# Gated recurrence, first two heads: where two weight splits stand on ScalarE, and where the second head's square sum stands on TensorE

## The reference, cut to what matters

```
def hgrn2_mixer(h, lb, w_in, o_norm, w_o):
    proj = h @ w_in
    q_x, f_x, i_x, g_x = jnp.split(proj, [HK, 2 * HK, 2 * HK + HV], axis=-1)
    f = lb + (1.0 - lb) * jax.nn.sigmoid(f_x)
    q = heads(jax.nn.silu(q_x)); k = heads(1.0 - f); log_f = heads(jnp.log(f)); v = heads(i_x)
    b = jnp.cumsum(log_f, axis=3)                    # chunks of 32 tokens
    q_rel = q * jnp.exp(b - b_ref);  k_rel = k * jnp.exp(b_ref - b)
    o_intra = (causal(q_rel k_rel^T)) v
    q_dec = q * jnp.exp(b);  k_dec = k * jnp.exp(b_last - b)
    # scan over chunks: o_inter = q_dec state; state = decay * state + k_dec^T v
    gate = silu(g_x)
    o = rms_norm(o_intra + o_inter, o_norm) * gate
    return o @ w_o
```

## Time and profile before

| | |
|---|---|
| median of 3 runs | 1789.33 us (1784.96, 1789.33, 1789.35) |
| the profiled execution | 1786.21 us |
| its span in the trace | 1784.2 us |
| PE busy | 1660.7 us, 93% of the span |
| the stretch that the change touches | 1091 to 1154 us |
| mean granted clock of PE | 0.968 of full speed |

### The profile page before, as it was taken

The page is one execution under the profiler, slowest core; times in us unless marked ns, Lnnn a source line. Parts: engine busy times, 40 slices in busy tenths (PEclk is TensorE's granted clock), DMA queues, the critical chain, the costliest instruction groups (busy, mean ns, idle before and its releaser), DMA issues.

```text
span 1784.2 us, 28711 instructions
## 1 busy us (share of the span) xinstructions
PE 1660.7 (93%) x10394; PEld 1345.7 (75%) x10394; DVE 850.8 (48%) x1463; ACT 744.1 (42%) x1149; POOL 648.7 (36%) x374
## 2 busy tenths in 40 slices
PE   5999979869889999999999999899999999999997
PEld 4787668837566668878888887788878878888885
DVE  6565868756675544532121245466664542212125
ACT  2333334323744444623142346567674622323232
POOL 5544310004421125644444453233334544444441
PEclk9999999979899999999999998799999999999997
DMA  8622210002121122233333331122222223333331
GB/s 291 194 83 74 69 37 3 4 12 83 47 60 28 33 71 83 72 95 93 98 92 105 94 104 39 48 71 59 73 69 84 59 83 94 99 91 105 94 95 59
DMA packets 250958, 140.33 MB, mean 79 GB/s; under 512 B 10122, under 2 KB 242657, under 8 KB 250865
## 3 DMA queue, kind: packets, MB, share of 16 engines
q1 hardware_dynamic: 249552, 137.12, 26.4%
q0 software_dynamic: 1008, 1.66, 0.4%
q10 hardware_dynamic: 304, 0.26, 0.0%
HBM read 136.93 MB, written 2.10 MB: 78 GB/s over the span
## 4 chain that ended last, share of the span: by engine, by line
issue 41%; PE 24%; POOL 11%; DVE 10%; ACT 5%; DVEq 4%; DMA 2%; ACTq 1%; POOLq 1%; SPq 1%
PE bank L745 13%; POOL w_low L554 10%; DVE hg_state L2046 2%; PE bank L1030 2%; DVE bank L2043 2%; PE bank L794 2%; DMA x_tok<-in_x 1%; DVEq L2479 1%; PE bank L1190 1%; PE bank L1189 1%; DVE hg_k_dec L2043 1%; DVEq L2792 1%; PE bank L1217 1%; SPq L438 1%; DVE sum_sq L2043 1%
## 5 line engine op out<-in xcount | busy, mean ns | idle before, releaser
L554 POOL TENSOR_TENSOR w_low<-w_raw,w_high 128x1024 fp32r<-128x1024 f32 (+2 forms) x218 | 517.5, 2374 | 989.7 <-ACT w_high L1476 989.6
L745 PE MATMUL bank<-act_high,w_high 128*128 128x512 f32 x976 | 392.8, 402 | 12.6 <-POOL w_low L554 10.5
L745 PE MATMUL bank<-act_low,w_high 128*128 128x512 f32 x976 | 383.5, 393 | 0.0
L745 PE MATMUL bank<-act_high,w_low 128*128 128x512 f32 x976 | 383.2, 393 | 0.0
L1476 ACT ACTIVATE w_high<-w_raw 128x1024 fp32r<-128x1024 f32 (+2 forms) x218 | 219.3, 1006 | 276.8 <-PE bank L745 265.3
L745 PEld LDWEIGHTS bank<-act_high,w_high 128*128 128x128 f32 x976 | 184.7, 189 | 66.1 <-POOL w_low L554 14.5
L745 PEld LDWEIGHTS bank<-act_high,w_low 128*128 128x128 f32 x976 | 184.7, 189 | 40.4
L745 PEld LDWEIGHTS bank<-act_low,w_high 128*128 128x128 f32 x976 | 185.0, 190 | 38.9 <-issue 2.2
L745 PE MATMUL bank<-hid_high,w_high 128*128 128x512 f32 x472 | 184.7, 391 | 3.8 <-DVE mix_out L2721 3.8
L745 PE MATMUL bank<-hid_low,w_high 128*128 128x512 f32 x472 | 184.4, 391 | 0.0
L745 PE MATMUL bank<-hid_high,w_low 128*128 128x512 f32 x472 | 184.4, 391 | 0.0
(11 more groups left out here) (566 smaller groups left out, 2869.8 us busy)
## 6 DMA issues: line engine op xcount, KB each, us to landing
w_raw<-in_mlp_w SPq DMA_DIRECT2D x128, 512.0 KB, 4.0
w_raw<-in_hgrn_w_in SPq DMA_DIRECT2D x32, 512.0 KB, 4.1
w_raw<-in_w_in SPq DMA_DIRECT2D x29, 512.0 KB, 4.0
w_ada_piece<-in_w_ada SPq DMA_DIRECT2D x5, 2048.0 KB, 16.2
w_raw<-in_w_out SPq DMA_DIRECT2D x8, 512.0 KB, 3.8
w_raw<-in_mla_w_o SPq DMA_DIRECT2D x8, 512.0 KB, 3.8
w_raw<-in_hgrn_w_o SPq DMA_DIRECT2D x8, 512.0 KB, 3.8
w_raw<-in_mla_w_in SPq DMA_DIRECT2D x6, 512.0 KB, 4.0
```

Source lines behind the costliest of these rows:

```text
L554: gp.tensor_tensor(WL[:, c0 % 2, 0:kt, 0:m], WR[:, c0 % 2, 0:kt, 0:m], WH[:, c0 % 2, 0:kt, 0:m].bitcast(F32), ALU.subtract).then_inc(w_lo, 1)
L745: mm = pe.matmul(bank[0:m, :], w[:, k, 0:m], a[:, k0 + k, :], start=(k == 0 and n_ == 0), stop=(k == kt - 1 and n_ == 2))
```

## The change

Three things are moved, and nothing is added or left out: the split of job G0+5 stands on ScalarE right behind that of G0+4, ahead of the norm's logarithm, where it stood behind the norm; the copy for G0+6 stands behind head 0's query silu, where it stood behind the five exponentials; and the square sum of head 0 stands amid job G0+7, after its first nine matmuls, where it stood behind the whole job. The loop over heads 2 to 7 is as before.

```
@@ job(c0, ..., amid=None)
                         mm = pe.matmul(bank[0:m, :], w[:, k, 0:m], a[:, k0 + k, :],
                                        start=(k == 0 and n_ == 0), stop=(k == kt - 1 and n_ == 2))
+                    if k == 2 and amid:
+                        amid()
                 mm.then_inc(job_done, 1)
@@ TensorE, hgrn(n, o, second)
-                if second:
-                    job(G0 + 3, n * 4, free["g"], n * 4 + 4)
-                if o is not None:
+                def square_sum():
                     pe.wait_ge(g_sq, o + 1)
                     pe.matmul(PB[7][:, :], ONES[:, :], OSQ[:, :], start=True, stop=True).then_inc(g_ss, 1)
+
+                if second:
+                    job(G0 + 3, n * 4, free["g"], n * 4 + 4, amid=square_sum)
+                elif o is not None:
+                    square_sum()
@@ ScalarE
             mlp(0, F0)
             high(G0 + 4)
+            high(G0 + 5)
             rstd_of(D, R1, 2)
 
             def hgrn(n, o, second=False):
 
-                if o is None:
-                    high(G0 + 5)
-                else:
+                if o is not None:
                     act.wait_ge(g_sc, o + 1)
...
                     act.activation(QG[:, :], TG[1][:, :], ACT.Silu).then_inc(g_sig, 1)
+                    if o is None:
+                        high(G0 + 6)
...
                     act.activation(GG[:, :], TG[3][:, :], ACT.Silu).then_inc(g_gate, 1)
-                if o is None:
-                    high(G0 + 6)
```

More of the change, by code:

```diff
@@ L733, in job @@
             def job(c0, r, fr, n, kt=8, m=P, hi=AH, lo=AL, k0=0, ready=None, bank=None,
-                    spare=None):
+                    spare=None, amid=None):
                 s = c0 % 2
```

## The result

The changed kernel takes 1776.51 us, the median of 4 runs (1772.66 to 1777.52), against 1787.14 us for the kernel before (4 runs, 1780.21 to 1789.35): a ratio of 0.9936, with a 95% interval from 0.9916 to 0.9957. Run again twice beside other kernels, with 12 runs each time, it gave 0.9944 [0.9926, 0.9963] and 0.9954 [0.9935, 0.9973]. As differences of medians that is 10.6, 8.6 and 7.2 us, where 8.6 was forecast.

A forecast was written before the change was run, and what follows sets the result against it. PE, busy 93% of the span, was taken to bound the kernel, through its waits and slowed clock. Terms 0.7 + 1.7 + 2.5 + 3.1 + 0.6 = 8.6 us, from 1787.5, gave 1778.9 us; range 1774 to 1785.5.

The forecast's parts named there:

- the third wait: PE's wait ahead of turning head 1's values: 2.8 us shrinks to 2.1; clock staying up gives up to 1.7.
- G0+5's start: PE starts G0+5 at 1104.7 us instead of 1105.38, released by VectorE's product instead of GpSimd's split: 0.7 us.
- the cover of the norm's table load: On ScalarE, G0+5's copy and the 1.28 us load finish before PE's sum, within 0.1 us; no cost to the norm.
- G0+5 at full clock: On PE, G0+5 takes 5.49 us instead of 7.16 behind a shorter wait: 1.7 us.
- the two nearest waits: PE's clock fell behind 2.03 us and stayed up behind 1.91, so 1.35 us ahead of G0+5 should keep it up.
- The wait ahead of G0+6: PE waits 0.9 us for GpSimd's low part instead of 3.41; G0+6 starts 2.5 us closer behind G0+5.
- G0+6 at full clock: On PE, G0+6 takes 5.49 us instead of 8.57 behind a short gap: 3.1 us.
- The square sum: Moved amid G0+7 on PE: Ln 1.0 us sooner, but VectorE's third product limits turning head 1's values: 0.6 us.
- the clock's: Rival: PE's clock falls all the same in G0+5 and G0+6; gain 6.0 us, 1781.5 us, chance 0.15.
- VectorE's last addition of squares: Rival: GpSimd's split shuts VectorE out of the norm's last addition; gain 3 to 6 us, some 1783.2 us, chance 0.08.
- The weights were there: Rival: G0+5's weights land late and its copy holds up the norm on ScalarE; slower, 1793 us, chance 0.02.
- Nothing was given back: Rival: weight loads or the loop behind the first heads take up the gain; no change, 1787.5 us, chance 0.05.

The follow-up runs named there:

- the table first: Changed kernel plus a one-column Ln on ScalarE ahead of G0+5's copy, so the norm's table loads before that copy; 0.9954 of before, 1775.72 us.
- the longer gap: Changed kernel with PE also waiting for head 0's logarithm ahead of G0+5; 1778.66 us against 1776.05 us for the changed kernel.
- the first two edits: Kernel before with G0+5's split ahead of the norm and G0+6's copy behind the silu, square sum not moved; 0.9948 of before.
- the first edit's profile: Kernel before with only G0+5's split moved ahead of the norm; 0.999 of before, 1780.84 us against 1783.15 us.
- the earlier copy: Changed kernel plus one-column Ln ahead of G0+5's copy, two VectorE products moved, G0+6's copy ahead of head 0's silu; 1771.65 us, again 1773.79 us.

## Why the prediction was right

The forecast was 8.6 us and its range held the time. The start from which the time was reckoned was partly luck: the kernel before had medians of 1787.14, 1783.15, 1783.94 and 1783.29 us in four sets of runs, and the forecast began at 1787.5. The stretch shrank by 8.5 us in one profile of the changed kernel and 9.8 in the two others; the 1.3 us between them are the clock behind the third wait, which the forecast had left to its range. By its steps:

- **G0+5's start**, 0.7 forecast, 0.33 measured. G0+5 is indeed released by VectorE's product. The step that was off is the cover of the norm's table load: the copy started at 1095.67, 0.42 us behind the end of G0+3's last matmul (1094.86 plus 0.39) and not 0.1 as reckoned. The load behind it made the norm's Ln 0.3 us late. The run with the table first gave that 0.3 back, though it also had the copy 0.3 us sooner. Where the 0.42 us come from stays open.
- **G0+5 at full clock**, 1.7 forecast, 1.6 measured; a full job takes 5.57 us up to the next step. The bound from the two nearest waits was a good guess, but not a rule: see the longer gap.
- **The wait ahead of G0+6**, 2.5 forecast, 2.9 measured: from G0+5's end to G0+6's start 1.14 us instead of 4.0. The forget gate took 0.55 us instead of 0.74, and PE was 0.3 us behind. So this miss and that of G0+5's start are in good part one: a PE that comes later finds a shorter wait.
- **G0+6 at full clock**, 3.1 forecast, 2.8 measured between starts. Taken together the scores come 7.6 us sooner, where 7.9 was forecast.
- **The square sum**, 0.6 forecast, 0.6 measured against before, with VectorE's third product as the thing that is late next. Against the first two edits it was 1.1 us and against the first edit's profile nothing: the 0.6 is right for a G0+7 at before's clock.
- **Behind the scores everything moved rigidly**: from there to G0+7's start it takes 13.6 us in every profile but those of the earlier copy (13.7).
- The **drain** of about 1.38 us that the Trainium skill adds to each table load (page "ScalarE: Activation LUTs", section "What ACT_TABLE_LOAD costs") did not show. By that estimate the Ln would have come at 1099.4; it came at 1098.05, 0.02 us behind the load, which itself stood 0.02 us behind the copy.
- Of the **rivals**, the clock's was wrong for the first two jobs in all three profiles of the changed kernel. VectorE's last addition of squares was not caught by GpSimd: it ended at 1096.52, and the subtraction began at 1096.81. The weights were there: G0+5's load was issued at 1089.5 and took 4.0 us, 1.7 us before the end of G0+3's last matmul. Nothing was given back.
- One sum is a little off: the early bound of the forecast's own range, G0+5 at half clock in place of the 0.9 us wait, is 8.6 less 1.7, plus 0.9, so 7.8 us and not 7.7. Nothing hangs on it.

What the sum did not show is how unequal the edits are. Each term had its place in the sum, but what the first edit wins up to G0+5's end, 1.9 us, hangs on the second: alone it gives 0.4.

## What to carry to other kernels

When several waits lie behind one another on the same engine, take out the last one first, or all: what an earlier one gives alone is waited away at the next. Price a wait of PE with the job behind it, because the clock that falls in the wait is paid by the matmuls after it, and leave a range, since the third wait of the changed kernel brought it down in one profile and not in two others; here 2.8 us came from filling the waits with work that nobody reads. And where a copy is put ahead of a change of function on ScalarE, and waits, the table load behind it is late by as much as the copy is; a one-column use of the function ahead of the copy went with 0.3 us here.

## What the runs showed of the hardware that I had not expected

- The granted clock behind a wait is not decided by the wait's length alone. Behind the ten waits of 0.3 to 1.8 us ahead of G0+5 and the four such third waits it was never down (judged by the 5.6 or 7.2 us of G0+5 and the 1.7 or 3 us behind the third wait). Of the four waits of 2.0 to 3.0 us ahead of G0+5 three brought it down (2.03, 2.04, 2.04) and 3.03 did not. Of the ten third waits of 2.4 to 3.0 us three left it up (2.83, 2.94, 2.98) and seven brought it down (2.41 to 2.76), so here it was the longest waits that left it up. In those three PE had got through G0+7 and whatever it had of the square sum soonest, 7.9 to 8.0 us from the job's start to the wait against 8.2 to 9.2 in the seven: the clock had come back earliest in the job before the wait. That is a pattern in ten profiles; no run was made to test it. All three waits of 3.36 us and more ahead of G0+6 brought it down.
- The spread of a kernel's own times is as large as the change. The start of the stretch, in front of which nothing is changed, lay between 1085.6 and 1094.5 us in the fourteen profiles, and the rest in two groups 3 us apart. Where the rest differs, in the one pair looked at, shows in the clock of two stretches of the same work (50 and 20 us long, around the second MLP's start), first in before, then in after:

```profile
1400.00:1450.00 50.00, 49.56 (x267) 0.94 0.22 64
1450.00:1470.00 20.00, 18.10 (x72) 0.91 0.27 79
```

```profile
1389.00:1439.00 50.00, 49.50 (x272) 0.97 0.22 64
1439.00:1459.00 20.00, 18.10 (x80) 1.00 0.35 102
```

  0.06 of 50 us and 0.09 of 20 are 4.8 us lost in before, 0.03 of 50 are 1.5 in after: 3.3 us, about the 3.1 by which the rests differ.
- The time from the modelled end of G0+3's last matmul to ScalarE's waiting copy for G0+5, while PE went on with the next job, took two values: 0.41 to 0.42 us in the six profiles where that copy stands right behind the copy for G0+4, and 0.09 to 0.10 us in the four where a table load and a one-column Ln stand between the two. Why is open.
